# A decoder step with routed experts: experts ranked by load on the chip, passes of 96, 64, 64, 128, 64, 96, 96 and 96 rows, and constant products in TensorE's routing waits

## The reference: what is computed

```python
def moe_swiglu(x, wr, br, w1, w3, w2):          # x: 264 rows of 1024; w1, w3, w2: 8 x 1024 x 1024, float32
    logits = (x @ wr) + br
    top_val, top_idx = lax.top_k(logits, 2)
    gates = jax.nn.softmax(top_val, axis=-1)
    combine = einsum('btk,btke->bte', gates, one_hot(top_idx, 8))
    for e in range(8):
        h = jax.nn.silu(x @ w1[e]) * (x @ w3[e])
        y = y + (combine[..., e:e + 1] * h) @ w2[e]
```

## Time and profile before

| what | value |
|---|---|
| median of 3 runs | 916.63 us (916.35 to 917.81) |
| profiled execution, its own time | 915.62 us |
| its span | 914.1 us |
| granted TensorE clock, mean | 0.956 of full |
| PE busy | 849.4 us (93%) |
| DVE, ACT, POOL busy | 253.8, 138.9, 97.1 us |
| DMA | 207.11 MB, 227 GB/s over the span |
| last product of the routing ends, expert passes begin | 600.3 us, 601.6 us |
| last expert product ends | 878.3 us |

### The profile page before, as it was taken

The page is one execution under the profiler, slowest core; times in us unless marked ns, Lnnn a source line. Parts: engine busy times, 40 slices in busy tenths (PEclk is TensorE's granted clock), DMA queues, the critical chain, the costliest instruction groups (busy, mean ns, idle before and its releaser), DMA issues.

```text
span 914.1 us, 14781 instructions
## 1 busy us (share of the span) xinstructions
PE 849.4 (93%) x6277; PEld 575.9 (63%) x6277; DVE 253.8 (28%) x707; ACT 138.9 (15%) x342; POOL 97.1 (11%) x143
## 2 busy tenths in 40 slices
PE   6999999999999999999989799799999999999940
PEld 5888778888888888867765668534343344344320
DVE  2173133000000000644777612632021021011118
ACT  0010113000000111312156611300010000000000
POOL 4300300000000000120314100021010010010130
PEclk9999999999999999999979899779999999999975
DMA  9899614455310378980234719469979999999532
GB/s 305 283 366 340 230 52 124 152 172 169 126 64 0 127 235 193 183 220 1 93 119 144 318 66 408 172 228 383 341 269 404 395 397 398 411 398 397 203 101 75
DMA packets 106737, 207.11 MB, mean 227 GB/s; under 512 B 23470, under 2 KB 60698, under 8 KB 105668
## 3 DMA queue, kind: packets, MB, share of 16 engines
q1 hardware_dynamic: 93492, 166.68, 52.1%
q0 software_dynamic: 9568, 33.19, 10.4%
q10 hardware_dynamic: 3632, 6.59, 2.1%
HBM read 192.97 MB, written 13.47 MB: 226 GB/s over the span
## 4 chain that ended last, share of the span: by engine, by line
PE 89%; DVE 6%; issue 1%; DMA 1%; ACT 1%; POOL 1%; SPq 0%; POOLq 0%; DVEq 0%; ACTq 0%
PE ps L646 43%; PE ps L1213 19%; PE ps L1202 10%; PE ps L697 3%; PE ps L1170 2%; PE ps L1033 1%; PE ps L976 1%; PE ps L984 1%; PE ps L1049 1%; PE ps L1195 1%; PE ps L1002 1%; PE ps L859 1%; PE ps L1016 1%; PE ps L1181 1%; DMA scr<-x_prompt 1%
## 5 line engine op out<-in xcount | busy, mean ns | idle before, releaser
L1213 PE MATMUL ps<-slot,hT 128*32 128x512 f32 x1600 | 174.9, 597 | 1.3 <-DVE hT L2043 1.3
L646 PE MATMUL ps<-rw,slot 128*128 128x264 f32 x640 | 142.6, 385 | 0.0
L646 PEld LDWEIGHTS ps<-rw,slot 128*128 128x128 f32 x640 | 120.8, 189 | 21.6
L1213 PEld LDWEIGHTS ps<-slot,hT 128*32 128x32 f32 x1600 | 51.8, 111 | 119.5 <-issue 116.8
L646 PE MATMUL ps<-xw,slot 128*128 128x264 f32 x512 | 121.2, 393 | 0.8 <-issue 0.8
L646 PEld LDWEIGHTS ps<-xw,slot 128*128 128x128 f32 x512 | 97.5, 193 | 19.6 <-issue 2.3
L1202 PE MATMUL ps<-slot,hT 128*32 128x256 f32 x1600 | 89.9, 380 | 0.0
L646 PE MATMUL ps<-hT,slot 128*128 128x264 f32 x352 | 79.7, 386 | 0.0
L646 PEld LDWEIGHTS ps<-hT,slot 128*128 128x128 f32 x352 | 66.3, 190 | 10.9
L1202 PEld LDWEIGHTS ps<-slot,hT 128*32 128x32 f32 x1600 | 50.3, 110 | 33.9 <-issue 1.7
L646 PE MATMUL ps<-yT,slot 128*128 128x264 f32 x256 | 59.4, 388 | 0.5 <-DVE yT L1924 0.5
(11 more groups left out here) (416 smaller groups left out, 796.8 us busy)
## 6 DMA issues: line engine op xcount, KB each, us to landing
slot<-moe_w SPq DMA_DIRECT2D x64, 1024.0 KB, 10.2
slot<-moe_w SPq DMA_DIRECT2D x16, 2048.0 KB, 12.0
slot<-ffn_w SPq DMA_DIRECT2D x22, 1024.0 KB, 8.3
slot<-ffn_w SPq DMA_DIRECT2D x8, 1408.0 KB, 6.8
slot<-w_in_even SPq DMA_DIRECT2D x4, 2048.0 KB, 15.1
r_rows<-silu ACTq DMA_DIRECT2D x1, 6144.0 KB, 31.8
slot<-w_out_even SPq DMA_DIRECT2D x2, 2048.0 KB, 24.2
slot<-w_in_odd SPq DMA_DIRECT2D x2, 2048.0 KB, 12.1
```

Of the source, the lines that this page charges most:

```text
L646: mm = pe.matmul(out, lhs(k), rhs(k), start=(k == 0), stop=(k == n - 1))
L1213: mm = pe.matmul(ps[t][32 * j:32 * j + 32, :].rearrange("p (w n) -> p w n", w=2), xgT[:, cap * k + 32 * t:cap * k + 32 * t + 32], moe_slab ...
```

## The change

Two things change.

**Ranks and pass sizes.** VectorE ranks experts 1 to 7 by their number of rows (ties by the lower number): `keyed` is the count less a sixteenth of the expert's number, `larger` compares all pairs, and the sum of a row of it is the rank. Rank 0 runs in pass 3 with 128 rows, ranks 4, 5 and 6 in passes 1, 2 and 4 with 64 (`THIN`), ranks 1, 2 and 3 in passes 5, 6 and 7 with 96. In tiles: 3, 2, 2, 4, 2, 3, 3, 3. A thin expert with more than 64 rows gets a further pass at the end. Passes 0 to 4 are now written out on each engine, the loop starts at 5. The operand layout of a thin pass stays that of 96 rows.

**Constant products.** `keep_busy(n)` has TensorE multiply the identity by a constant of 256 columns n times into an unused PSUM bank: nine times before its wait for `chosen`, twice before its wait for `sel_ready`.

```diff
+        THIN = 64
         def tiles_at(i):
-            return (0, 3, 7)[i] if isinstance(i, int) else 3 * i + 1
+            return (0, 3, 5, 7, 11, 13)[i] if isinstance(i, int) else 3 * i - 2
         def rows_at(i):
-            return (0, CAP)[i] if isinstance(i, int) and i < 2 else CAP * i + WIDE - CAP
+            return CAP * i if isinstance(i, int) and i < 4 else CAP * i + WIDE - CAP
...
# SyncE
-            with sp.Fori(2, n) as i:
+            for i in range(2, 5):
+                next_expert(i)
+            with sp.Fori(5, n) as i:
                 next_expert(i)
# GpSimd
-            pool.dma_start(xg, r_rows[CAP:CAP + WIDE, :]).then_inc(xg_in, 16)
+            pool.dma_start(xg[0:CAP], r_rows[CAP:2 * CAP, :]).then_inc(xg_in, 16)
             one_pass(0, 3)
-            one_pass(1, 4)
+            one_pass(1, 2, WIDE)
+            one_pass(2, 2)
+            one_pass(3, 4)
+            one_pass(4, 2)
# TensorE
+            def keep_busy(n):
+                for _ in range(n):
+                    pe.matmul(ps[2][:, 0:2 * P], ident, square[:, 1:3, :].rearrange("p a q -> p (a q)"), start=True, stop=True)
+            keep_busy(9)
             pe.wait_ge(chosen, 1)
...
+            keep_busy(2)
             pe.wait_ge(sel_ready, 1)
...
-                base, cap = tiles_at(i), 32 * nt
-                turned = (3, 7, 3) if nt == 3 else (2, 3, 2, 3)
+                base, cap = tiles_at(i), max(32 * nt, CAP)
+                turned = (3, 7, 3) if nt < 4 else (2, 3, 2, 3)
...
-            one_pass(0, 3, WIDE)
-            one_pass(1, 4, CAP)
-            with pe.Fori(2, n) as i:
+            one_pass(0, 3, CAP)
+            one_pass(1, 2, CAP)
+            one_pass(2, 2, WIDE)
+            one_pass(3, 4, CAP)
+            one_pass(4, 2, CAP)
+            with pe.Fori(5, n) as i:
# VectorE
-            link(V.tensor_copy(cntw, counts))
-            link(V.memset(cntw[:, 0:1], -1.0))
-            link(V.max(out=topw, in_=cntw))
-            link(V.max_index(widx, topw, cntw))
-            link(V.tensor_copy(wf, widx[:, 0:1]))
...
+            link(V.scalar_tensor_tensor(out=keyed, in0=iota8, scalar=-1.0 / 16, in1=counts, op0=ALU.mult, op1=ALU.add))
+            link(V.memset(keyed[:, 0:1], -1.0))
+            link(V.tensor_tensor(larger, keyed.unsqueeze(1).to_broadcast([P, NE, NE]),
+                                 keyed.unsqueeze(2).to_broadcast([P, NE, NE]), ALU.is_gt))
+            link(V.tensor_reduce(out=rank, in_=larger, axis=AX, op=ALU.add))
+            mark(V.tensor_scalar(wide32, rank, 0.0, float(WIDE - CAP), ALU.is_equal, ALU.mult))
+            mark(V.tensor_scalar(basew, rank, float(CAP), float(4 * CAP + WIDE - CAP - 1), ALU.mult, ALU.add))
+            link(V.tensor_scalar(thin32, rank, 4.0, float(CAP - THIN), ALU.is_ge, ALU.mult))
...
+            link(V.tensor_tensor(match, at_pass.unsqueeze(1).to_broadcast([1, 16, 24]),
+                                 iotac[0:1, 0:16].unsqueeze(2).to_broadcast([1, 16, 24]), ALU.is_equal))
+            link(V.tensor_tensor(match, match, iota24[0:1, :].unsqueeze(1).to_broadcast([1, 16, 24]), ALU.mult))
+            link(V.tensor_reduce(out=listed, in_=match, axis=AX, op=ALU.add))
+            V.tensor_copy(qlist[:], listed).then_inc(list_ready, 1)
```

More of the change, by code:

```diff
@@ L140, in build @@
         npass = sb("npass", [1, 1], I32)
-        iota8 = sb("iota8", [P, 8])
+        iota24 = sb("iota24", [P, 24])
+        iota8 = iota24[:, 0:8]
         iotac = sb("iotac", [P, CAP])
@@ L214, in build @@
         over_f, over_p = scr[:, 2400:2416], scr[:, 2416:2432]
-        over_n = scr[0:1, 2448:2453]
-        over_m = scr[0:1, 2464:2544].rearrange("p (i q) -> p i q", i=5)
         far1, far2 = scr[:, 2560:2568], scr[:, 2568:2576]
-        cntw, topw, isw, cumw = (scr[:, 2576 + 8 * a:2584 + 8 * a] for a in range(4))
-        basew, slack = scr[:, 2608:2616], scr[:, 2616:2624]
-        widx = mxi[:, 0, :]
-        wf, wrow_ = scr[:, 2624:2625], scr[:, 2625:2626]
+        keyed, rank, wide32, thin32 = (scr[:, 2576 + 8 * a:2584 + 8 * a] for a in range(4))
+        basew, slack, late = (scr[:, 2608 + 8 * a:2616 + 8 * a] for a in range(3))
+        larger = scr[:, 2688:2752].rearrange("p (a e) -> p a e", a=NE)
+        at_pass = scr[0:1, 2752:2776]
+        listed = scr[0:1, 2816:2832]
+        match = scr[0:1, 2832:3216].rearrange("p (i q) -> p i q", i=16)
+        sixth = scr[:, 2632:2640]
         beyond = scr[:, 2640:2664].rearrange("p (t e) -> p t e", t=3)
@@ L607, in _ @@
             one_pass(0, 3)
-            one_pass(1, 4)
+            one_pass(1, 2, WIDE)
+            one_pass(2, 2)
+            one_pass(3, 4)
+            one_pass(4, 2)
             pool.wait_ge(passes_ready, 1)
             n = pool.value_load(npass[0:1, 0:1], min_val=NE, max_val=MAXP)
-            with pool.Fori(2, n) as i:
+            with pool.Fori(5, n) as i:
                 one_pass(i, 3)
@@ L1307, in _ @@
             act.wait_ge(even_tc, 2)
-            act.wait_ge(pool_consts, 6)
+            act.wait_ge(pool_consts, 5)
             norm(4, vT, vT, V_SG, V_SB)
@@ L1494, in _ @@
             one_pass(0, 3)
-            one_pass(1, 4)
-            with act.Fori(2, n) as i:
+            one_pass(1, 2)
+            one_pass(2, 2)
+            one_pass(3, 4)
+            one_pass(4, 2)
+            with act.Fori(5, n) as i:
                 one_pass(i, 3)
@@ L1996, in _ @@
-            dve.wait_ge(dchain, chain.k)
-            mark(V.tensor_scalar(slack, isw, float(WIDE - CAP), None, ALU.mult))
-            mark(V.tensor_scalar(basew, isw, wrow_, None, ALU.mult))
-            link(V.scalar_tensor_tensor(out=cumw, in0=cumw, scalar=float(-CAP), in1=rowb[:], op0=ALU.mult, op1=ALU.add))
-            mark(V.tensor_tensor(basew, cumw, basew, ALU.subtract))
-            link(V.tensor_tensor(cntw, counts, slack, ALU.subtract))
-            link(V.memset(basew[:, 0:1], -1.0))
@@ L2003, in _ @@
-            mark(V.tensor_scalar(over_f[:, 0:8], cntw, float(CAP), None, ALU.is_gt))
-            mark(V.tensor_scalar(over_f[:, 8:16], cntw, 2.0 * CAP, None, ALU.is_gt))
-            mark(V.tensor_tensor(tmp8[:], place[:], by_tile(basew), ALU.add))
+            link(V.scalar_tensor_tensor(out=keyed, in0=iota8, scalar=-1.0 / 16, in1=counts, op0=ALU.mult, op1=ALU.add))
+            link(V.memset(keyed[:, 0:1], -1.0))
+            link(V.tensor_tensor(larger, keyed.unsqueeze(1).to_broadcast([P, NE, NE]),
+                                 keyed.unsqueeze(2).to_broadcast([P, NE, NE]), ALU.is_gt))
@@ L2006, in _ @@
+            link(V.scalar_tensor_tensor(out=basew, in0=wide32, scalar=-1.0 - CAP / (WIDE - CAP), in1=basew,
+                                        op0=ALU.mult, op1=ALU.add))
+            link(V.tensor_tensor(basew, basew, sixth, ALU.add))
+            mark(V.scalar_tensor_tensor(out=basew, in0=thin32, scalar=-1.0 - 7 * CAP / (CAP - THIN), in1=basew,
+                                        op0=ALU.mult, op1=ALU.add))
+            link(V.tensor_tensor(slack, wide32, thin32, ALU.subtract))
             mark(V.tensor_tensor(beyond, place[:], by_tile(slack), ALU.subtract))
-            mark(V.tensor_tensor(far2, slack, basew, ALU.add))
@@ L2008, in _ @@
-            dve.wait_ge(dchain, chain.k)
+            link(V.tensor_tensor(keyed, counts, slack, ALU.subtract))
+            mark(V.tensor_scalar(over_f[:, 0:8], keyed, float(CAP), None, ALU.is_gt))
+            link(V.tensor_scalar(over_f[:, 8:16], keyed, 2.0 * CAP, None, ALU.is_gt))
             link(V.tensor_tensor_scan(over_p, over_f, over_f, 0.0, ALU.add, ALU.bypass))
             V.tensor_scalar(npass[:], over_p[0:1, 15:16], float(NE), None, ALU.add).then_inc(passes_ready, 1)
+            link(V.memset(basew[:, 0:1], -1.0))
@@ L2011, in _ @@
+            mark(V.tensor_tensor(tmp8[:], place[:], by_tile(basew), ALU.add))
+            link(V.tensor_tensor(far2, slack, basew, ALU.add))
             link(V.scalar_tensor_tensor(out=far1, in0=over_p[:, 0:8], scalar=float(CAP), in1=far2,
@@ L2074, in one_pass @@
                     V.tensor_copy(orow[:, t, :], ps[4 + t][:, 0:256]).then_inc(o_free, 1)
-            one_pass(0, 3, WIDE)
-            one_pass(1, 4, CAP)
+            one_pass(0, 3, CAP)
+            one_pass(1, 2, CAP)
+            one_pass(2, 2, WIDE)
+            one_pass(3, 4, CAP)
+            one_pass(4, 2, CAP)
             dve.wait_ge(passes_ready, 1)
             n = dve.value_load(npass[0:1, 0:1], min_val=NE, max_val=MAXP)
-            with dve.Fori(2, n) as i:
+            with dve.Fori(5, n) as i:
                 one_pass(i, 3, CAP)
```

48 lines of the change are left out of this document (21 added, 27 removed).

## The result

| | before | after |
|---|---|---|
| median of runs on the same chip | 916.82 us (916.35 to 917.81, 4 runs) | 890.99 us (887.05 to 892.30, 4 runs) |
| ratio to before, 95% interval | | 0.971 (0.968 to 0.974) |
| profiled execution, its span | 915.62, 914.1 us | 892.3, 890.7 us |
| first product of the passes | 601.62 us | 599.71 us |
| first product's start to last product's end | 276.7 us | 255.3 us |

The kernel is 25.8 us faster, where 32 were forecast. The runs after are spread over 5 us, and the profiled execution (892.30 us) is the slowest of the four; experiment k shows a part of what is behind that. First the page: busy time by engine, the chain that ended last, the costliest group, and the weight loads (KB each, median us from issue to landing).

The account below looks back on a forecast made before the run. TensorE bounds the passes, with the DMA engines just as full. Net -5.7 us at the start, -30.2 from thin passes and +4.0 for weights make 32 us less: 883.6, plus 1.0 for the median, 884.5 us; range 878 to 894.

Parts of the forecast that it names:

- rival 1: Routing: the clock falls before or in the count, first product at 602.5, 891 us in all; chance 0.24.
- signs of being wrong: Clock 0.50 in the gather, weight waits nothing or over 8 us, first product later than 598, or over eight passes.
- Thin passes: The three passes of 64 rows: each takes 22.8 us on TensorE, a gain of 10.05 each, -30.2 us together.
- Constant products: Routing: they fill TensorE's idle time; if the clock holds at 1.00, count takes 1.6 us and gather 7.1.
- The mixture: Routing: the clock falls halfway through the gather, 887 us or so; counted within rival 1's chance of 0.24.
- VectorE's list: Before the passes: next to be late, first copy 8.6 us after the tables' start, so first product at 595.4.
- The weights: Passes 1 to 7: queue full at 402 GB/s, 33.26 us an expert, end 4.0 us after TensorE's own.
- 17.4 us behind slot 3: Last pass: slot 3's slab, landing at 829.0, binds; 17.4 us of work behind it give the end at 846.4.
- None of it in the wide pass: Passes: TensorE's waits for weight loads, 4 us together, were to leave out the pass of 128 rows.
- Rival 2: Passes: the weights never hold TensorE, products end at 842.4, 880.5 us in all; chance 0.11.
- Rival 3: Passes: the weight queue is slower under load, 375 to 395 GB/s, 888 to 901 us in all; chance 0.12.
- Rival 4: Passes: thin experts over 64 rows cost further passes, 33.3 us each, 918 or 951 us; chance 0.03.

Follow-up runs that it names:

- k: The changed kernel measured a second time, nothing altered: 888.32 us, ratio 0.970 to the kernel before.
- a: The changed kernel without the constant products, so ranks and pass sizes alone: 893.86 us, ratio 0.975 to the kernel before.
- c: The changed kernel with more constant products, five inside the count and eight inside the gather: 890.42 us, ratio 0.973 to the kernel before.
- h: The changed kernel with e's last pass, f's late list and a few constant products inside count and gather: 892.41 us, ratio 0.975 to the kernel before.
- j: The changed kernel with e's last pass and f's late list, no constant products inside count or gather: 884.80 us, ratio 0.965 to the kernel before.
- d: The changed kernel with half of slot 5's weight slab left unloaded for experts 1 to 7 (results wrong): 881.51 us, ratio 0.962 to the kernel before.
- f: The changed kernel with VectorE's list of experts worked out behind the copies of expert 0's rows: 888.98 us, ratio 0.971 to the kernel before.
- e: The changed kernel with 64 rows in the last pass, passes 5 to 7 written out, no code for further passes: 885.36 us, ratio 0.967 to before.
- b: The kernel before with the constant products added and nothing else: 912.09 us, ratio 0.996 to the kernel before.
- i: The changed kernel with e's last pass and c's constant products inside count and gather: 885.50 us, ratio 0.965 to the kernel before.

## Why the prediction was right and where not

The direction, the mechanism of the gain and its order were right: 884.5 forecast, 890.99 measured, inside 878 to 894. The time is rival 1's 891, but that match is luck: rival 1 has the first product 2.8 us later than it came and the weights at 4.0 us, where they cost 7.1 to 8.7. Two of the prediction's own signs of being wrong came true: the clock reads 0.50 in the gather, and the first product starts at 599.71, later than 598.

- **Thin passes, -10.05 us each: right.** 22.84 us against 22.8 in passes 1 and 4; pass 2, ahead of the wide one, takes 23.6 without its 2.2 us of waits, by the wide pass's longer transposes and the restarts.
- **Constant products, "If that holds the clock at 1.00": right for the count, wrong for the gather.** This is the step that failed most. The count took 2.00 (1.6 forecast), the gather 13.34 and not 7.1. I had reasoned from idle time alone: 4.32 us cost the clock, so under 1 us should keep it. In 586 to 590 us there is no idle time at all and the clock is 0.50, and in a it fell only 0.4 us into the wait. Rival 1 had the clock fall before or in the count; it fell in the gather, and its time for the start of the first product, 602.5, was 2.8 us too late. The mixture that the prediction puts with rival 1, in which the clock falls halfway through the gather (887 or so), is what k shows in one execution (profiled at 888). The Trainium skill, "TensorE: Matmul & The Clock Gate", section "A second HAM failure mode", puts such swings down to small idle spells between groups. They don't suffice here: the fall at 586.0 came with 3.85 of 4.00 us busy ahead of it, the one at 590.3 in k with 4.00 of 4.00. What differs between the gather and c is the kind of products. But that narrow products are the cause is not shown: in h and j the clock fell while products of 256 columns were running (for 0.3 and 0.8 us by then).
- **VectorE's list: its length right, its place wrong.** 8.70 us against 8.6; but with the gather ending at 598.4 instead of 591.65 it was 3.7 us early. First product at 599.71 instead of 595.4: 4.3 us of the missing gain. Even in d, at 19.55 us after the router, the gather was last: it ended at 593.61, and the first product came at 594.94.
- **The weights, +4.0 us: the mechanism right, the size too small.** The queue was at 398 to 410 GB/s with 402 taken, and the last slab landed 239.7 us after the first issue, 236.8 forecast. But d puts the price at 8.7 us, and at 7.1 against k. Two things were missed. I worked out the wait of the last pass alone. TensorE waited instead in pass 2 and ahead of the wide pass, where two thin passes stand behind each other, and waited 5.4 us. And I gave a wait no price beyond its length: within the 3.18 us the clock fell, for 6.8 us, which cost the wide first product 2.8 (1.4 in k). In the last three passes of this profile slabs land 0.9 to 3 us early, so the "17.4 us behind slot 3" did not decide; in k it is a slab of the last pass that binds, by 0.18 us. "None of it in the wide pass" was wrong too: the longest wait is the one that opens it.
- **Sum.** 4.3 us in the start and 4.3 us in the passes are the 8.6 us between the forecast 32 and the 23.4 of the profiled execution. That execution is the slowest of the four; the median misses the forecast by 6.5 us, the fastest (887.05) by 2.6. The tail, 35.7 us, is as before.
- **Rival 2** is refuted by the three waits, and its time is seen when d takes them away: 881.5 measured, 880.5 worked out. Rival 3's cause, a slower queue, is not what happened. Rival 4 did not occur: eight passes ran.

**Open.** What decides where the clock falls was not found. In kernels with the same constant products ahead of it, it fell in two groups behind the start of the router's products: 7.8 to 8.9 us (j, f, after) and 12.5 to 13.0 us (k, e, b, d), and the same program has both. Products of other widths in place of the gather's might tell it, and were not run.

## What to carry to other kernels

Cutting TensorE's work in passes that stream weights pays less once a pass is shorter than its load (22.8 against an estimated 33.3 us here: of 30.2 us cut, a kept 22.4); from there on work out the arrival for every pass, in order, and not only for the last one, and count a wait as its length plus what the clock takes behind it. Constant products in a wait are worth their while when they stand in idle time (b: -4.2 us for 11 products); between other products they ate what they won (c, i), and where they didn't hold the clock both were lost (h). Before pricing what is "next to be late", check that the step ahead of it will really speed up.

## What the runs showed of the hardware

- The granted clock fell with TensorE busy: at 590.3 us in k with 4.00 of 4.00 us busy ahead, at 586.0 us (after) with 3.85 of 4.00, both in products of 96 columns behind those of 8. With products of 256 columns between them it held in c and i (one profile each), but in h and j it fell while such products ran. Where it falls moves between executions of one program: 1.0 and 4.8 us into the gather.
- It also fell in the passes, at 685.0 us within a wait of 3.18 us, shortly after one of 0.73 (busy 2.94 of 5.00), and in e at 829.0 us, right behind a wait of 2.38 us. In a it fell 0.4 us after TensorE's last product, before the change 3.7 us after it.
- One core's DMA engines held 398 to 410 GB/s over 33 us with share 1.03 (402 before). The Trainium skill, "DMA: Bandwidth & Descriptors", section "Measured", gives 425 GB/s, which no long stretch here reached. At that load loads of 1 and 2 MB land 18.5 and 22.5 us after issue (medians), up from 10.2 and 12.0, and SyncE's instruction that issues one takes 1.96 us (median) instead of 0.37.
